# Two views, 64 bytes apart, of the normalised and inner rows of a two-block transformer kernel

## The chip, the cores and the metric

The kernel runs as one program on one core of a Trainium2 chip. The metric is device time in microseconds of one execution. The kernel before took 2518.12 us, the median of 3 runs that lay between 2514.95 and 2522.17 us.

## The reference, cut to what matters

All arithmetic is float32. There are 1024 model columns and 256 tokens per stream. A first block works on one stream ("b1" in the kernel). Two further layers ("l0", "l1") work on that stream and on a context stream of 256 tokens together, 512 tokens in all, until the last phases, in which the context is no longer needed. Each block is a gated feed-forward part, a mixer, and a second gated feed-forward part, each behind an RMS norm with modulation:

```python
D_MODEL = 1024; SEQ = 256; D_FF = 2816

def rmsnorm(x, g):
    xf = x.astype(jnp.float32)
    y = xf * lax.rsqrt(jnp.mean(xf * xf, axis=-1, keepdims=True) + NORM_EPS)
    return (y * g.astype(jnp.float32)).astype(x.dtype)
def modulate(x, shift, scale):
    return x * (1 + scale[:, None, :]) + shift[:, None, :]
def swiglu(x, w_gu, w_down):
    g, u = jnp.split(x @ w_gu, 2, axis=-1)
    return (jax.nn.silu(g) * u) @ w_down
...
    mod = c_act @ w_ada[l] + b_ada[l]
    (sh1, sc1, gt1, sh2, sc2, gt2, sh3, sc3, gt3) = jnp.split(mod, N_MOD, axis=-1)
    y = modulate(rmsnorm(h, norm_ffn1[l]), sh1, sc1)
    h = h + 0.5 * gt1[:, None, :] * swiglu(y, w_ffn1_gu[l], w_ffn1_down[l])
    y = modulate(rmsnorm(h, norm_mix[l]), sh2, sc2)
    proj = y @ w_in[l]
    ...  # attention and a gated MLP in b1, windowed attention and a long filter in l0, retention in l1
    h = h + gt2[:, None, :] * (merged @ w_out[l])
    y = modulate(rmsnorm(h, norm_ffn2[l]), sh3, sc3)
    h = h + 0.5 * gt3[:, None, :] * swiglu(y, w_ffn2_gu[l], w_ffn2_down[l])
```

Nearly all of the work is the products with the weight matrices: w_gu (1024 x 5632), w_down (2816 x 1024) twice per block, w_in and w_out.

## The kernel before, in words

Activations lie transposed in SBUF: 128 partitions are 128 model columns, and the free dimension is tokens. A product therefore has a 128 x 128 block of weights as its stationary operand and a row of 256 or 512 tokens as its moving operand, and its result goes to a PSUM tile (`pg`). To keep float32 accuracy with the faster float32r matmuls, every operand is split in two: a high part (`whi`, `Yh`, `Hh`) and the remainder (`wlo`, `Yl`, `Hl`). The helper `three` issues three matmuls for each block, one each at lines 1159, 1160 and 1161: high weights times high row, high weights times low row, low weights times high row. In the value blocks of the mixers the roles are exchanged (`three_moving`, lines 1335 to 1337): the weights are the moving operand with 256 columns, and 128 tokens of `Yh` or `Yl` are the stationary one.

The table `PHASES` orders the work in 18 phases, with a kind, a number of weight blocks and a number of tokens for each:

```python
PHASES = [
    ("b1_gu1", "t", 22, 256), ("b1_down1", "d", 16, 256),
    ("b1_in", "m", 10, 256), ("b1_out", "t", 4, 256),
    ("b1_gu2", "t", 22, 256), ("b1_down2", "d", 16, 256),
    ("l0_gu1", "t", 22, 512), ("l0_down1", "d", 16, 512),
    ("l0_in", "m", 12, 512), ("l0_out", "t", 4, 512),
    ("l0_gu2", "t", 22, 512), ("l0_down2", "d", 16, 512),
    ("l1_gu1", "t", 22, 512), ("l1_down1", "d", 16, 512),
    ("l1_in", "m", 24, 512), ("l1_out", "r", 8, 256),
    ("l1_gu2", "t", 22, 256), ("l1_down2", "d", 16, 256),
]
```

A block of kind "t" is 8 depth slices by 2 column halves by 3 matmuls, 48 in all; so are the blocks of the mixer inputs ("m", where a value block over 512 tokens has 96) and of "r". A block of kind "d" (`w_down`) is 11 depth slices by 3, 33 matmuls. "t" and "m" phases read the normalised rows `Yh` and `Yl` (8 rows of 512 columns each), "d" phases read the inner rows `Hh` and `Hl` (22 rows of 512 columns each), and l1_out reads `OH` and `OL`. A phase of 256 tokens uses the first 256 columns of a row. Every row starts 2048 bytes behind the one before it.

Weights travel so: SyncE issues the DMA of a block into one of two `raw` buffers (1 MB, or 704 KB for "d"), ScalarE rounds it to `whi` (lines 662, 667), VectorE subtracts to give `wlo` (lines 2049, 2054), and TensorE waits for `lo_ready`. ScalarE also writes `Yh` (line 710) and `Hh` (line 682), VectorE writes `Yl` (line 2209) and GpSimd `Hl` (line 526). Semaphore counts written out in each engine's program set the whole order; there is no scheduler. Between the weight blocks VectorE computes the modulation vectors from `w_ada` (line 2089).

Addresses: all tiles are laid out one behind another by `sb`, by hand. `X`, `Yh`, `Yl`, `raw`, `whi`, `wlo` and `ada` are multiples of 8192 bytes per partition. `V` (410 columns, 1664 bytes with its rounding), `MOD` (1728), and the small tiles up to `small` follow; `at[0] += 64` ahead of `region` makes up for `MOD`, so that `region`, with `Hh` and `Hl` in it, lies a multiple of 128 bytes behind `X`. Everything from line 241 on reuses `region` for the mixers (`over()` sets the address back).

Of the kernel before, what the change touches and what calls it, by code (L numbers as in the profile page):

```python
# [184 lines left out]

READS = {"b1_gu1": "b1_0", "b1_in": "b1_1", "b1_out": "merge", "b1_gu2": "b1_2", "l0_gu1": "l0_0", "l0_in": "l0_1",
# [3 lines left out]
def two_blocks(nc, x_t, ctx_t, vec, w_t, w_d, w_ada, emb_t, fw1, fw23, fw4, window, dft, rope1, sgu_w, sgu_b,  # L190
# [15 lines left out]
    Yh = sb("Yh", [P, 4096], F32R)  # L206
    Yl = sb("Yl", [P, 4096], F32R)
    raw = sb("raw", [P, 2, BLK])
# [18 lines left out]
    Hh = sb("Hh", [P, KF, 512], F32R)  # L227
    Hl = sb("Hl", [P, KF, 512], F32R)

# [4 lines left out]
    HF = nc.alloc_sbuf_tensor_at("HF", [P, 8, 512], F32, offset=y_at)[:, :, 256:512]  # L234
    DF0 = nc.alloc_sbuf_tensor_at("DF0", [P, 8, 512], F32, offset=y_at + 16384)[:, 2:6, 256:512]
    taps = nc.alloc_sbuf_tensor_at("HP", [P, 22, 512], F32, offset=region)
# [28 lines left out]
    over()  # L265
    k3_at = at[0]
# [28 lines left out]
    Yh8, Yl8, Yh16, Yl16 = rhs_t(Yh), rhs_t(Yl), rhs_r(Yh), rhs_r(Yl)  # L295
# [17 lines left out]
    with ExitStack() as ctx:  # L313
# [166 lines left out]
        def _(pool):  # L480
# [30 lines left out]
            def hidden_lo(name):  # L511

                tokens = INFO[name][2]
                k = FFNS.index(name) * KF
                if name == "b1_gu2":
                    for m in range(KF):
                        pool.wait_ge(sem["h_hi"], k + m + 1)
                        pool.tensor_tensor(Hl[:, m, 0:tokens], TMP[:, m % 2, 0:tokens], Hh[:, m, 0:tokens].bitcast(F32), ALU.subtract)\
                            .then_inc(sem["h_lo"], 1)
                        if m >= 4 and m < 19:  # L520
                            ctx_squares(m - 4)
                    return
                with pool.Fori(0, KF // 2) as j:
                    for u in range(2):
                        pool.wait_ge(sem["h_hi"], j * 2 + (k + u + 1))
                        pool.tensor_tensor(Hl[:, bass.ds(j * 2 + u, 1), 0:tokens], TMP[:, u:u + 1, 0:tokens],  # L526
                                           Hh[:, bass.ds(j * 2 + u, 1), 0:tokens].bitcast(F32), ALU.subtract)\
                            .then_inc(sem["h_lo"], 1)
# [107 lines left out]
        def _(act):  # L636
# [35 lines left out]
            def gate_evac(name):  # L672
# [4 lines left out]
                def evac(j, u):  # L677
# [4 lines left out]
                    act.activation(Hh[:, bass.ds(j * 2 + u, 1), 0:tokens], TMP[:, u:u + 1, 0:tokens], ACT.Copy)\  # L682
# [3 lines left out]
            def norm(name, chunks_of, tokens, shift, post, following=None):  # L686
# [20 lines left out]
                for c in range(k):  # L707
                    act.wait_ge(sem["scaled"], base + c + 1)
                    for s, cols in streams(tokens):
                        ins = act.activation(Yh8[:, c + post, cols], TMP[:, c % 2, cols], ACT.Identity, bias=shift(c, s)) \  # L710
                            if shift else act.activation(Yh8[:, c + post, cols], TMP[:, c % 2, cols], ACT.Copy)
# [5 lines left out]
            def lead_norm(name, shift, following):  # L717
# [8 lines left out]
                for c in range(k):  # L726
                    act.wait_ge(sem["lead_dve"], lead_dve(name, "scaled", c))
                    act.activation(Yh8[:, c, 0:256], TMP[:, c % 2, 0:256], ACT.Identity, bias=shift(c, 0)).then_inc(sem["lead_act"], 1)
# [15 lines left out]
            def rest_hi(name, shift, chunks):  # L744

                for c in chunks:
                    act.wait_ge(sem["scaled"], NORMS[name][1] + c + 1)
                    act.activation(Yh8[:, c, 256:512], TMP[:, c % 2, 256:512], ACT.Identity, bias=shift(c, 1)).then_inc(sem["y_hi"], 1)
# [219 lines left out]
            for c in range(8):  # L968
                act.wait_ge(sem["scaled"], base + c + 1)
                act.activation(Yh8[:, c, 0:256], TMP[:, c % 2, 0:256], ACT.Copy).then_inc(sem["y_hi"], 1)  # L970
# [184 lines left out]
        def _(pe):  # L1155
# [83 lines left out]
            def lead_products(name, u, n, signal):  # L1239

                def part(kt, half, cols):
                    w = slice(256 * kt + P * half, 256 * kt + P * half + P)
                    return three(pg[u][:, half, cols], whi[:, n % 2, w], wlo[:, n % 2, w], Yh8[:, kt, cols], Yl8[:, kt, cols], kt == 0, kt == 7)
# [13 lines left out]
            def lead_blocks(name, phase):  # L1257
# [9 lines left out]
                def other(kt, half, cols):  # L1267
                    w = slice(256 * kt + P * half, 256 * kt + P * half + P)
                    return three(pg[1][:, half, cols], whi[:, 1, w], wlo[:, 1, w], Yh8[:, kt, cols], Yl8[:, kt, cols], kt == 0, kt == 7)
# [13 lines left out]
            def product(name, first=0):  # L1283
# [4 lines left out]
                if mode == "d":  # L1288
                    h_before = KF * [f.replace("gu", "down") for f in FFNS].index(name) + CREDIT
# [212 lines left out]
            def b1_half(i):  # L1502
# [7 lines left out]
                for kt in range(8):  # L1510
                    if kind == "v":
                        w = slice(256 * kt, 256 * kt + 256)
                        y = slice(P * (i % 2), P * (i % 2) + P)
                        last = three_moving(out, whi[:, u, w], wlo[:, u, w], Yh8[:, kt, y], Yl8[:, kt, y], kt == 0, kt == 7)
                    else:
                        w = slice(256 * kt + P * (i % 2), 256 * kt + P * (i % 2) + P)
                        last = three(out, whi[:, u, w], wlo[:, u, w], Yh8[:, kt, 0:256], Yl8[:, kt, 0:256], kt == 0, kt == 7)
                last.then_inc(sem["b1_half"], 1)

            def b1_first_halves():  # L1520
# [3 lines left out]
                for kt in range(8):  # L1524
                    pe.wait_ge(sem["y_lo"], y_before("b1_1") + kt + 1)
                    for half in range(2):
                        w = slice(256 * kt + P * half, 256 * kt + P * half + P)
                        last = three(pg[0][:, half, 0:256], whi[:, b1_base % 2, w], wlo[:, b1_base % 2, w],
                                     Yh8[:, kt, 0:256], Yl8[:, kt, 0:256], kt == 0, kt == 7)
# [386 lines left out]
            def l1_block(b):  # L1916
# [12 lines left out]
                if kind == "v":  # L1929
                    for tt in range(4):  # L1930
                        out = pg[u][:, tt // 2, 256 * (tt % 2):256 * (tt % 2) + 256]
                        for kt in range(8):
                            w, y = slice(256 * kt, 256 * kt + 256), slice(P * tt, P * tt + P)
                            last = three_moving(out, whi[:, u, w], wlo[:, u, w], Yh8[:, kt, y], Yl8[:, kt, y], kt == 0, kt == 7)
                else:
                    tokens = 512 if kind == "k" else 256
                    for kt in range(8):
                        for half in range(2):
                            w = slice(256 * kt + P * half, 256 * kt + P * half + P)
                            last = three(pg[u][:, half, 0:tokens], whi[:, u, w], wlo[:, u, w],  # L1940
                                         Yh8[:, kt, 0:tokens], Yl8[:, kt, 0:tokens], kt == 0, kt == 7)
# [90 lines left out]
        def _(dve):  # L2032
# [160 lines left out]
            def norm(name, chunks_of, tokens, gain, shift, post, following=None):  # L2193
# [10 lines left out]
                def lo(c):  # L2204
                    dve.wait_ge(sem["y_hi"], yb + c + 1)
                    for s, cols in streams(tokens):
                        hi_part = Yh8[:, c + post, cols].bitcast(F32)
                        if shift:
                            ins = dve.scalar_tensor_tensor(Yl8[:, c + post, cols], TMP[:, c % 2, cols], shift(c, s), hi_part,  # L2209
                                                           ALU.add, ALU.subtract)  # L2210
                        else:
                            ins = dve.tensor_tensor(Yl8[:, c + post, cols], TMP[:, c % 2, cols], hi_part, ALU.subtract)
# [15 lines left out]
            def lead_norm(name, gate, gain, shift, following):  # L2228
# [8 lines left out]
                def lo(c):  # L2237
                    dve.wait_ge(sem["lead_act"], lead_act(name, "hi", c))
                    dve.scalar_tensor_tensor(Yl8[:, c, 0:256], TMP[:, c % 2, 0:256], shift(c, 0), Yh8[:, c, 0:256].bitcast(F32),
# [748 lines left out]
```

## Time and profile before

| | |
|---|---|
| median of 3 runs | 2518.12 us |
| the profiled execution's own time | 2518.71 us |
| its span | 2516.9 us |
| mean granted TensorE clock | 0.984 of 2.4 GHz |
| TensorE busy with matmuls | 2442.9 us (97%), 14736 matmuls |
| VectorE, ScalarE, GpSimd busy | 1515.5, 893.3, 380.7 us |
| share of the chain that ended last | TensorE 85%, VectorE 7%, ScalarE 3%, DMA 3% |

[...]

### The profile page before, as it was taken

How to read it: one execution, taken by the hardware profiler on the slowest of the kernel's cores; microseconds unless marked ns; L12 is line 12 of the kernel's file. 1: busy time of each engine (PE TensorE's matmuls, PEld its weight loads, DVE VectorE, ACT ScalarE, POOL GpSimd, SP SyncE). 2: the span in 40 equal slices, each digit the busy share in tenths (PEclk: the TensorE clock that was granted, in tenths of full speed). 3: DMA queues.
4: the chain of work that ended last, by engine and by line, in shares of the span. 5: the costliest groups of instructions: out<-in, count | busy, mean ns of one | idle time of the engine just before them, and what ended most of it. 6: DMA issues, size and time to landing. Idle time of an engine off the chain costs nothing.

```text
span 2516.9 us, 39335 instructions
## 1 busy us (share of the span) xinstructions
PE 2442.9 (97%) x14736; PEld 2165.5 (86%) x14736; DVE 1515.5 (60%) x2434; ACT 893.3 (35%) x1103; POOL 380.7 (15%) x353
## 2 busy tenths in 40 slices
PE   6999989999999998999999999999999999999999
PEld 5998879999888888867778888888888889999999
DVE  7676767967877765355477776642222364555444
ACT  4443554444222223332232222232222242254443
POOL 2110531211111102332211111001110001000110
PEclk7999989999999999999999999999999999999999
DMA  7877745854655554211135545422222342234545
GB/s 279 277 260 268 260 140 199 272 196 167 209 192 200 175 167 153 80 63 51 67 119 198 197 170 191 161 101 89 94 84 97 104 143 84 68 118 151 184 168 166
DMA packets 79878, 400.19 MB, mean 159 GB/s; under 512 B 8816, under 2 KB 12912, under 8 KB 54704
## 3 DMA queue, kind: packets, MB, share of 16 engines
q1 hardware_dynamic: 77216, 393.39, 45.3%
q0 software_dynamic: 1056, 3.67, 0.4%
q10 hardware_dynamic: 1520, 1.95, 0.2%
q8 instruction: 58, 0.95, 0.2%
q14 instruction: 28, 0.23, 0.0%
HBM read 396.88 MB, written 2.10 MB: 159 GB/s over the span
## 4 chain that ended last, share of the span: by engine, by line
PE 85%; DVE 7%; ACT 3%; DMA 3%; issue 2%; POOL 0%; ACTq 0%; SPq 0%; DVEq 0%; POOLq 0%
PE pg L1159 24%; PE pg L1161 24%; PE pg L1160 24%; DMA raw<-w_d 2%; PE pg L1335 2%; PE pg L1336 2%; PE pg L1337 2%; DVE wlo L2049 1%; PE px L1977 1%; DMA raw<-w_t 1%; ACT whi L662 1%; DVE ada L2089 1%; PE px L1738 1%; PE pg L1777 1%; PE px L1963 1%
## 5 line engine op out<-in xcount | busy, mean ns | idle before, releaser
L1159 PE MATMUL pg<-Yh,whi 128*128 128x256 f32 (+1 forms) x2856 | 958.6, 336 | 27.5 <-DVE Yl L2209 7.6
L1160 PE MATMUL pg<-Yl,whi 128*128 128x256 f32 (+1 forms) x2856 | 948.5, 332 | 0.0
L1161 PE MATMUL pg<-Yh,wlo 128*128 128x256 f32 (+1 forms) x2856 | 948.3, 332 | 0.0
L2054 DVE TENSOR_TENSOR wlo<-raw,whi 128x2048 fp32r<-128x2048 f32 (+1 forms) x202 | 415.0, 2055 | 517.7 <-ACT whi L667 517.0
L1159 PEld LDWEIGHTS pg<-Yh,whi 128*128 128x128 f32 x2856 | 548.0, 192 | 90.4 <-issue 20.9
L1161 PEld LDWEIGHTS pg<-Yh,wlo 128*128 128x128 f32 x2856 | 548.1, 192 | 50.1
L1160 PEld LDWEIGHTS pg<-Yl,whi 128*128 128x128 f32 x2856 | 548.4, 192 | 49.0
L667 ACT ACTIVATE whi<-raw 128x2048 fp32r<-128x2048 f32 (+1 forms) x202 | 348.4, 1725 | 563.8 <-PE pg L1161 521.8
L1159 PE MATMUL pg<-Hh,whi 128*128 128x256 f32 (+1 forms) x1122 | 368.9, 329 | 4.7 <-DVE wlo L2054 3.2
L1160 PE MATMUL pg<-Hl,whi 128*128 128x256 f32 (+1 forms) x1122 | 366.4, 327 | 0.0
L1161 PE MATMUL pg<-Hh,wlo 128*128 128x256 f32 (+1 forms) x1122 | 366.4, 327 | 0.0
L526 POOL TENSOR_TENSOR Hl<-TMP,Hh 128x512 f32 (+1 forms) x110 | 117.9, 1072 | 912.7 <-ACT Hh L682 912.7
L2089 DVE CUSTOM_DVE_ANT_0 ada<-ada,px 128x1024 f32<-128x1024 f32 x200 | 243.7, 1218 | 13.9 <-DMA ada<-w_ada 8.5
L1159 PEld LDWEIGHTS pg<-Hh,whi 128*128 128x128 f32 x1122 | 213.2, 190 | 25.6 <-DVE wlo L2054 5.1
L1160 PEld LDWEIGHTS pg<-Hl,whi 128*128 128x128 f32 x1122 | 213.3, 190 | 18.1
L1161 PEld LDWEIGHTS pg<-Hh,wlo 128*128 128x128 f32 x1122 | 213.3, 190 | 17.9
L2049 DVE TENSOR_TENSOR wlo<-raw,whi 128x2048 fp32r<-128x2048 f32 (+1 forms) x65 | 132.9, 2044 | 115.6 <-ACT whi L662 115.5
L662 ACT ACTIVATE whi<-raw 128x2048 fp32r<-128x2048 f32 (+1 forms) x63 | 107.7, 1709 | 237.0 <-PE pg L1161 116.7
L682 ACT ACTIVATE Hh<-TMP 128x256 f32 (+3 forms) x132 | 69.4, 525 | 341.9 <-DVE TMP L2162 341.9
L568 POOL TENSOR_TENSOR wlo<-raw,whi 128x512 fp32r<-128x512 f32 x88 | 111.9, 1302 | 177.1 <-ACT whi L982 124.7
L495 POOL TENSOR_TENSOR TMP<-TMP,SQ 128x512 f32<-128x512 f32 (+1 forms) x54 | 58.7, 1088 | 387.2 <-ACT SQ L773 322.5
L2086 DVE CUSTOM_DVE_ANT_0 RS<-ada,px,small 128x512 f32<-128x512 f32 x144 | 107.7, 748 | 5.1
(352 smaller groups left out, 2354.8 us busy)
## 6 DMA issues: line engine op xcount, KB each, us to landing
raw<-w_t SPq DMA_DIRECT2D x194, 1024.0 KB, 5.0
ada<-w_ada SPq DMA_DIRECT2D x200, 512.0 KB, 3.6
raw<-w_d SPq DMA_DIRECT2D x96, 704.0 KB, 4.1
ADA<-w_ada SPq DMA_DIRECT2D x16, 512.0 KB, 14.6
NB<-na_bias POOLq DMA_DIRECT2D x8, 256.0 KB, 2.9
X<-x_t ACTq DMA_DIRECT2D x2, 512.0 KB, 16.7
spectrum<-HF POOLq DMA_DIRECT2D x1, 1024.0 KB, 9.2
X<-ctx_t SPq DMA_DIRECT2D x1, 1024.0 KB, 7.4
```

The source lines that it names most:

```text
L526: pool.tensor_tensor(Hl[:, bass.ds(j * 2 + u, 1), 0:tokens], TMP[:, u:u + 1, 0:tokens], Hh[:, bass.ds(j * 2 + u, 1), 0:tokens].bitcast(F32 ...
L568: ins = pool.tensor_tensor(wlo[:, n % 2, part], raw[:, n % 2, part], whi[:, n % 2, part].bitcast(F32), ALU.subtract)
L662: act.activation(whi[:, n % 2, 0:size], raw[:, n % 2, 0:size], ACT.Copy).then_inc(sem["hi_ready"], 1)
L667: act.activation(whi[:, n % 2, 0:size], raw[:, n % 2, 0:size], ACT.Copy).then_inc(sem["hi_ready"], 1)
L682: act.activation(Hh[:, bass.ds(j * 2 + u, 1), 0:tokens], TMP[:, u:u + 1, 0:tokens], ACT.Copy)\
L1159: pe.matmul(out, w_hi, y_hi, start=first, stop=False)
L1160: pe.matmul(out, w_hi, y_lo, start=False, stop=False)
L1161: return pe.matmul(out, w_lo, y_hi, start=False, stop=last)
L2049: dve.tensor_tensor(wlo[:, n % 2, 0:size], raw[:, n % 2, 0:size], whi[:, n % 2, 0:size].bitcast(F32), ALU.subtract)\
L2054: dve.tensor_tensor(wlo[:, n % 2, 0:size], raw[:, n % 2, 0:size], whi[:, n % 2, 0:size].bitcast(F32), ALU.subtract)\
L2086: summed(dve.tensor_tensor_reduce(RS[:, :], ada[:, n % 2, 512:1024], px[1][:, 1, :], 1.0, part, ALU.mult, ALU.add, total[:, 0:1]), 2)
L2089: summed(dve.tensor_tensor_reduce(w, w, px[2 - streams][:, :, :], 1.0, 0.0, ALU.mult, ALU.add, total[:, streams - 1:streams]), 1 if stream ...
```

## The change

`Yh`, `Yl`, `Hh` and `Hl` each get a second view, 64 bytes further on (`YhB`, `YlB`, `HhB`, `HlB`). `row_view` and `inner_of` give the later view to the phases of 256 columns (and to the whole of l1_in, whose key blocks have 512 columns), and the earlier view to the others. The tiles of the l1 mixer, `OH` and `OL` among them, begin 64 bytes later as well, and so do the tiles of the filter taps (`HF`, `DF0`, `HP`). 128 bytes of padding stand behind `Yh`, `Yl` and `Hh`, 64 behind `Hl`; what follows moves by 128 or 256 bytes. No instruction is added, removed or moved on any engine, and no semaphore count changes.

```diff
+SHORT_ROWS = ("b1_0", "b1_gu1", "b1_1", "b1_in", "merge", "b1_out", "b1_2", "b1_gu2", "l1_1", "l1_in", "l1_2", "l1_gu2")
...
     y_at = at[0]
     Yh = sb("Yh", [P, 4096], F32R)
+    YhB = nc.alloc_sbuf_tensor_at("YhB", [P, 4096], F32R, offset=y_at + 64)
+    at[0] += 128
+    yl_at = at[0]
     Yl = sb("Yl", [P, 4096], F32R)
+    YlB = nc.alloc_sbuf_tensor_at("YlB", [P, 4096], F32R, offset=yl_at + 64)
+    at[0] += 128
...
     Hh = sb("Hh", [P, KF, 512], F32R)
+    HhB = nc.alloc_sbuf_tensor_at("HhB", [P, KF, 512], F32R, offset=region + 64)
+    at[0] += 128
+    hl_at = at[0]
     Hl = sb("Hl", [P, KF, 512], F32R)
+    HlB = nc.alloc_sbuf_tensor_at("HlB", [P, KF, 512], F32R, offset=hl_at + 64)
+    at[0] += 64
+    assert at[0] <= end
...
-    HF = nc.alloc_sbuf_tensor_at("HF", [P, 8, 512], F32, offset=y_at)[:, :, 256:512]
+    HF = nc.alloc_sbuf_tensor_at("HF", [P, 8, 512], F32, offset=y_at + 64)[:, :, 256:512]
...
     over()
+    at[0] += 64
     k3_at = at[0]
...
+    def row_view(name):
+        return (YhB8, YlB8) if name in SHORT_ROWS else (Yh8, Yl8)
+    def inner_of(name):
+        return (HhB, HlB) if INFO[name][2] == 256 else (Hh, Hl)
...
                                     last = three(pg[v][:, 0, 0:tokens], whi[:, half, w], wlo[:, half, w],
-                                                 Hh[:, 11 * half + kt, 0:tokens], Hl[:, 11 * half + kt, 0:tokens],
+                                                 inner_hi[:, 11 * half + kt, 0:tokens], inner_lo[:, 11 * half + kt, 0:tokens],
                                                  half == 0 and kt == 0, half == 1 and kt == 10)
...
                                 last = three(pg[u][:, half, 0:tokens], whi[:, u, w], wlo[:, u, w],
-                                             Yh8[:, kt, 0:tokens], Yl8[:, kt, 0:tokens], kt == 0, kt == 7)
+                                             row_view(name)[0][:, kt, 0:tokens], row_view(name)[1][:, kt, 0:tokens], kt == 0, kt == 7)
```

The writers (ScalarE, VectorE, GpSimd) and every other reader of these rows get the same replacement.

## Rows read from the trace of the kernel before

**Rows 1.** The page: chain that ended last, by engine and by line.
```profile
PE 85%; DVE 7%; ACT 3%; DMA 3%; issue 2%; POOL 0%; ACTq 0%; SPq 0%; DVEq 0%; POOLq 0%
```
**Rows 2.** PE by stretch: us, busy (x records), granted clock, DMA share, GB/s.
```profile
60.00:100.00 40.00, 40.00 (x335) 1.00 0.82 278
60.00:180.00 120.00, 120.00 (x1002) 1.00 0.78 269
640.00:700.00 60.00, 60.00 (x266) 1.00 0.61 210
640.00:940.00 300.00, 300.00 (x1325) 1.00 0.55 188
2360.00:2400.00 40.00, 40.00 (x336) 1.00 0.51 179
2360.00:2480.00 120.00, 120.00 (x1003) 1.00 0.51 175
190.00:250.00 60.00, 55.35 (x428) 1.00 0.78 267
250.00:420.00 170.00, 153.47 (x1074) 0.92 0.54 192
```
**Rows 3.** Matmul groups by shape, whole run: line, names, shapes, count, busy, mean ns.
```profile
L1160 PE MATMUL pg<-Yl,whi 128*128 128x256 f32 x1584 | 453.4, 286 | 0.0
L1160 PE MATMUL pg<-Hl,whi 128*128 128x256 f32 x660 | 186.7, 283 | 0.0
L1337 PE MATMUL pg<-whi,Yl 128*128 128x256 f32 x352 | 99.6, 283 | 0.0
L1160 PE MATMUL pg<-OL,whi 128*128 128x256 f32 x128 | 36.2, 283 | 0.0
```
**Rows 4.** Timeline of PE just after a wait: start us, length us, instruction.
```profile
272.43 0.35 PE L1159 MATMUL pg<-Yh,whi 128*128 128x256 f32 x1 [1.20 <-POOL wlo L568]
272.62 0.28 PE L1160 MATMUL pg<-Yl,whi 128*128 128x256 f32 x1
272.74 0.28 PE L1161 MATMUL pg<-Yh,wlo 128*128 128x256 f32 x1
272.85 0.28 PE L1159 MATMUL pg<-Yh,whi 128*128 128x256 f32 x1
272.97 0.28 PE L1160 MATMUL pg<-Yl,whi 128*128 128x256 f32 x1
...
273.45 0.28 PE L1161 MATMUL pg<-Yh,wlo 128*128 128x256 f32 x1
```
**Rows 5.** Timeline of PE at a block's boundary in b1_gu1.
```profile
54.40 0.29 PE L1159 MATMUL pg<-Yh,whi 128*128 128x256 f32 x1
54.53 0.28 PE L1160 MATMUL pg<-Yl,whi 128*128 128x256 f32 x1
54.66 0.29 PE L1161 MATMUL pg<-Yh,wlo 128*128 128x256 f32 x1
54.78 0.28 PE L1159 MATMUL pg<-Yh,whi 128*128 128x256 f32 x1
```
**Rows 6.** Timeline of PE before 51 us, at the lower granted clock.
```profile
48.75 0.41 PE L1159 MATMUL pg<-Yh,whi 128*128 128x256 f32 x1
...
50.46 0.41 PE L1161 MATMUL pg<-Yh,wlo 128*128 128x256 f32 x1
```
**Rows 7.** Timeline of PE in the l1 mixer: ten float32 matmuls, merged.
```profile
2194.98 2.32 PE L1977 MATMUL px<-G,VN 128*128 128x256 f32 x10
```
**Rows 8.** Weight loads (PEld) by shape in 60:190 us.
```profile
L1160 PEld LDWEIGHTS pg<-Yl,whi 128*128 128x128 f32 x321 | 61.6, 192 | 0.0
```
**Rows 9.** The same in 640:940 us, beside matmuls of 512 columns.
```profile
L1161 PEld LDWEIGHTS pg<-Yh,wlo 128*128 128x128 f32 x300 | 56.3, 188 | 11.6
```
**Rows 10.** The chain that ended last, in order of time, in b1_down1.
```profile
210.19 5.68 DMA raw<-w_d
215.97 1.39 ACT whi L667
217.38 1.64 DVE wlo L2054
219.18 5.57 DMA raw<-w_d
```
**Rows 11.** Waits of ScalarE in 60:170 us: us in total, times, longest us.
```profile
ACT whi L667 <- PE pg L1161: 12.2, 19, 0.7
```

More of the change, by code:

```diff
@@ L709, in norm @@
                     for s, cols in streams(tokens):
-                        ins = act.activation(Yh8[:, c + post, cols], TMP[:, c % 2, cols], ACT.Identity, bias=shift(c, s)) \
-                            if shift else act.activation(Yh8[:, c + post, cols], TMP[:, c % 2, cols], ACT.Copy)
+                        ins = act.activation(row_view(name)[0][:, c + post, cols], TMP[:, c % 2, cols], ACT.Identity, bias=shift(c, s)) \
+                            if shift else act.activation(row_view(name)[0][:, c + post, cols], TMP[:, c % 2, cols], ACT.Copy)
                     ins.then_inc(sem["y_hi"], 1)
@@ L727, in lead_norm @@
                     act.wait_ge(sem["lead_dve"], lead_dve(name, "scaled", c))
[L728 removed]
+                    act.activation(row_view(name)[0][:, c, 0:256], TMP[:, c % 2, 0:256], ACT.Identity, bias=shift(c, 0)).then_inc(sem["lead_act"], 1)
                     if c == 3:
@@ L747, in rest_hi @@
                     act.wait_ge(sem["scaled"], NORMS[name][1] + c + 1)
-                    act.activation(Yh8[:, c, 256:512], TMP[:, c % 2, 256:512], ACT.Identity, bias=shift(c, 1)).then_inc(sem["y_hi"], 1)
+                    act.activation(row_view(name)[0][:, c, 256:512], TMP[:, c % 2, 256:512], ACT.Identity, bias=shift(c, 1)).then_inc(sem["y_hi"], 1)
             def squares(name):
@@ L1242, in part @@
                     w = slice(256 * kt + P * half, 256 * kt + P * half + P)
-                    return three(pg[u][:, half, cols], whi[:, n % 2, w], wlo[:, n % 2, w], Yh8[:, kt, cols], Yl8[:, kt, cols], kt == 0, kt == 7)
+                    return three(pg[u][:, half, cols], whi[:, n % 2, w], wlo[:, n % 2, w], row_view(name)[0][:, kt, cols], row_view(name)[1][:, kt, cols], kt == 0, kt == 7)
                 for kt in range(8):
@@ L1268, in other @@
                     w = slice(256 * kt + P * half, 256 * kt + P * half + P)
-                    return three(pg[1][:, half, cols], whi[:, 1, w], wlo[:, 1, w], Yh8[:, kt, cols], Yl8[:, kt, cols], kt == 0, kt == 7)
+                    return three(pg[1][:, half, cols], whi[:, 1, w], wlo[:, 1, w], row_view(name)[0][:, kt, cols], row_view(name)[1][:, kt, cols], kt == 0, kt == 7)
                 for kt in range(8):
@@ L1513, in b1_half @@
                         y = slice(P * (i % 2), P * (i % 2) + P)
-                        last = three_moving(out, whi[:, u, w], wlo[:, u, w], Yh8[:, kt, y], Yl8[:, kt, y], kt == 0, kt == 7)
+                        last = three_moving(out, whi[:, u, w], wlo[:, u, w], row_view("b1_in")[0][:, kt, y], row_view("b1_in")[1][:, kt, y], kt == 0, kt == 7)
                     else:
                         w = slice(256 * kt + P * (i % 2), 256 * kt + P * (i % 2) + P)
-                        last = three(out, whi[:, u, w], wlo[:, u, w], Yh8[:, kt, 0:256], Yl8[:, kt, 0:256], kt == 0, kt == 7)
+                        last = three(out, whi[:, u, w], wlo[:, u, w], row_view("b1_in")[0][:, kt, 0:256], row_view("b1_in")[1][:, kt, 0:256], kt == 0, kt == 7)
                 last.then_inc(sem["b1_half"], 1)
@@ L1528, in b1_first_halves @@
                         last = three(pg[0][:, half, 0:256], whi[:, b1_base % 2, w], wlo[:, b1_base % 2, w],
-                                     Yh8[:, kt, 0:256], Yl8[:, kt, 0:256], kt == 0, kt == 7)
+                                     row_view("b1_in")[0][:, kt, 0:256], row_view("b1_in")[1][:, kt, 0:256], kt == 0, kt == 7)
                         if kt == 7:
@@ L1933, in l1_block @@
                             w, y = slice(256 * kt, 256 * kt + 256), slice(P * tt, P * tt + P)
-                            last = three_moving(out, whi[:, u, w], wlo[:, u, w], Yh8[:, kt, y], Yl8[:, kt, y], kt == 0, kt == 7)
+                            last = three_moving(out, whi[:, u, w], wlo[:, u, w], row_view("l1_in")[0][:, kt, y], row_view("l1_in")[1][:, kt, y], kt == 0, kt == 7)
                 else:
@@ L1940, in l1_block @@
                             last = three(pg[u][:, half, 0:tokens], whi[:, u, w], wlo[:, u, w],
-                                         Yh8[:, kt, 0:tokens], Yl8[:, kt, 0:tokens], kt == 0, kt == 7)
+                                         row_view("l1_in")[0][:, kt, 0:tokens], row_view("l1_in")[1][:, kt, 0:tokens], kt == 0, kt == 7)
                 last.then_inc(sem["pe_block"], 1)
```

30 lines of the change are left out of this document (16 added, 14 removed).

## The prediction

> **What bounds the kernel now.** I read the chain of work that ended last before all else, since busy shares say little in an engine that overlaps its own work. TensorE holds 85% of it, and no other engine more than 7% [rows 1]. So the price of one matmul decides, and the record's length does not give it, because records overlap. I took it from the counts in two windows that differ by a known stretch. In the 256-column phases 120 us hold 667 more records than 40 us: 80,000 / 667 = 119.94 ns from start to start. In the last phase, the same lengths again give 667. The DMA share is 0.78 in the first and 0.51 in the last, so the load of the DMA engines does not set this period. With 512 columns it is 240,000 / 1059 = 226.6 ns [rows 2].
>
> At the full granted clock, 2.4 GHz, 256 columns take 106.7 ns and 512 take 213.3 ns. Both periods therefore lie 13.3 ns above the streaming time. At the lower level, 1.2 GHz, eight matmuls from 48.75 to 50.46 us are 213.8 ns apart [rows 6], which is 256 / 1.2 and nothing more: the 13.3 ns show only at the full clock. The float32 matmuls of the l1 mixer stream 256 columns twice. Ten of them take 2.32 us, and with a record of 0.379 us for the last, nine distances of 215.7 ns: 2.4 ns above 213.3 [rows 7]. So the engine can start a matmul 2.4 ns behind the last column of the one before; the float32r ones do not.
>
> **Is any of the 13.3 ns movable by an address?** Two rows say a part may be. First, the period of 256-column matmuls is not always 119.94 ns. After a wait, the starts at 272.62, 272.74, 272.85 and 272.97 are 117 ns apart on average, and seven distances up to 273.45 average 118.6 ns [rows 4]. Operands, shapes and clock are those of the steady stretch. Something takes hold after a few matmuls and costs some 2.5 ns each. Second, a weight load has a record of 192 ns beside 256-column matmuls and 188 ns beside 512-column ones [rows 8, 9], though both load the same 128 x 128 block. The stream of the row and the load of the next weights start within nanoseconds of each other and read the same memory at addresses that all agree modulo 128 bytes: by the code `Yh`, `Yl`, `Hh`, `Hl`, `whi` and `wlo` are multiples of 128 behind one another, and their slices step by 512 or 2048 bytes. The change shifts one of the two streams by 64 bytes in the 256-column phases and leaves the 512-column phases, in which the load is not stretched, as they are. That is a case for a gain, not a proof: no float32r row of before starts at another phase.
>
> A rule of the Trainium skill speaks against this reading. "TensorE: Matmul & The Clock Gate", Part 2, step 1, has it that the moving operand and the weight load have independent read ports, and that loading weights takes no bandwidth from the running matmul. By that rule the two records would be alike; the 192 beside the 188 ns [rows 8, 9] do not agree with it. With it the sum would be nothing, 2518 us.
>
> **Part by part.** No instruction comes, goes or moves, so no wait and no queue changes; only addresses do.
>
> (a) Moving operands shifted by 64 bytes. From the phase table: b1_gu1 and b1_gu2 22 x 48 = 1056 each; b1_down1 and b1_down2 16 x 33 = 528 each; b1_in without its two value blocks 8 x 48 = 384; b1_out 192; l1_in's four q and eight g blocks 576; l1_out 384; l1_gu2 1056; l1_down2 528. Sum 6288, out of 3 x (1584 + 660 + 128) = 7116 records with a row of 256 columns [rows 3]; the rest belong to 512-token phases that work in halves.
>
> Of these, b1_down1 (528) and b1_in (384) stand between waits. In 190 to 250 us TensorE is busy only 55.35 of 60 us, in 250 to 420 us 153.47 of 170 [rows 2]. In b1_down1 the chain runs through load, rounding and subtraction (5.68 + 1.39 + 1.64 us, then the next load) without TensorE [rows 10], so a shorter matmul there only lengthens the wait. That leaves 5376 on the path. In b1_gu1, beside the highest DMA share, ScalarE waits for TensorE before each rounding, 12.2 / 19 = 0.64 us [rows 11]. A block that is 48 x 2.4 ns = 0.12 us shorter stays under that, so the loads are next but not yet late.
>
> Price of one: bounded below by the float32 row, which would make the period 106.7 + 2.4 = 109.1 ns, a gain of 10.8 ns, 5376 x 10.8 = 58 us. Bounded above by the longest distances that stand in a row without a wait: 54.40 to 54.78 us, three distances of 126.7 ns [rows 5], a loss of 6.8 ns, 37 us on 5376. I take 117.5 ns, what the engine does before the slower pattern takes hold [rows 4], between the 117 of the first three distances and the 118.6 of seven: a gain of 2.44 ns. 5376 x 2.44 = 13.1 us.
>
> (b) Value blocks of b1_in and l1_in: 96 + 768 = 864 matmuls keep the weights as their moving operand and now load `Yh` or `Yl` from the shifted view. Their record is like the others' (283 ns, [rows 3]). If the phase between the two streams is what matters they gain 2.44 ns as well, 2.1 us; if the row's own start does, nothing. I take nothing.
>
> (c) The key blocks of l1_in, 4 x 48 = 192 matmuls of 512 columns, read the shifted view. By the ends of (a), 10.8 ns gained to 6.8 lost, they are worth -2.1 to +1.3 us; I take 0, as [rows 9] show nothing stretched there.
>
> (d) The 128 and 256 bytes of padding move `whi`, `wlo`, `raw`, `ada` and the rest by multiples of 128. For the 512-column phases this keeps every phase modulo 128 (`Yl` and `Hl` change modulo 256 against `Yh`). Nothing in the rows separates 128 from 256; bounds as in (a) on 5202 matmuls of 512 columns would be -56 to +35 us. I take 0, because the only pattern that I see is the one of the shared phase, and I leave this inside the range.
>
> (e) float32 matmuls of the l1 mixer with operands 64 bytes later: already at 2.4 ns above streaming [rows 7], so a gain is at most 2.4 ns each, under 1 us for about 300. Writes of ScalarE, VectorE and GpSimd to shifted rows: their time is hidden behind TensorE except in the norms, where a chunk is 0.4 to 0.5 us; I take 0.
>
> Sum: -13.1 us against the profiled execution's own 2518.71 us (span 2516.9), 0.6 us above the median of the runs. From the median: 2518.1 - 13.1 = 2505 us.
>
> **Rivals.** *Nothing changes.* The start address is immaterial at this grain; 117 ns after a wait is only a queue being refilled, and 192 beside 188 ns a matter of overlap. For it: the steady period is 119.94 in three tiles alike (`Yh`, `Hh`, `OH`), and no row shows an address at work. Time 2518 us. The Trainium skill's "SBUF — State Buffer" page, section on the DMA port swizzle, knows only 16-byte lines, which a shift by 64 bytes does not touch; by that rule, too, the time stays at 2518 us. No row here separates it from this rival.
>
> *A deep gain.* Most of the 13.3 ns is a matter of the start address, and the period falls to 109 to 115 ns. For it: the float32 row at 2.4 ns. Against it: the 512-column period carries the same 13.3 ns though its weight load is not stretched, so the bulk looks like a fixed cost of float32r. At 112 ns, 5376 x 7.9 = 43 us, 2475 us; less if the rounding in the b1 phases then comes late, since 48 x 7.9 = 0.38 us nears the 0.64 of [rows 11].
>
> *The loads take it back.* The 2.44 ns are there, but in b1_gu1, b1_gu2 and b1_down2 (2640 matmuls) the weights become the bound as in b1_down1. What is left is 2736 x 2.44 = 6.7 us: 2511 us. Against it: the 0.64 us of slack.
>
> *Slower.* The shifted row meets the weight load in a worse phase, or spans one more line of memory at each end, and the period rises to the 126.7 ns of [rows 5] in the shifted phases: +37 us on the 5376, 2555 us. It decides from 121.3 ns on (1.4 ns x 5376 = 7.6 us). For it: such distances exist. Against it: they are three in a row at one block's boundary, after which 120 returns.
>
> **How the numbers follow.** A difference under 0.3%, 7.6 us, is about what a measurement of this kernel cannot tell from none. Chances: the forecast 0.38 (its own range 2498 to 2512), deep gain 0.17, nothing 0.27, taken back 0.05, slower 0.13. Nearly all of the first two is faster than 2510.5 us: 0.54. Within 0.3%: the rest of the forecast, nothing and taken back, 0.33. Slower 0.13. The range 2470 to 2524 us leaves out the far end of the deep gain, with the bounds of (d) that go with it, and most of the slower case.
>
> **What would show it.** Right: in 60 to 180 us against 60 to 100 us, about 681 more records in place of 667 (117.5 ns), the same in 2360 to 2480, and in 640 to 940 still 1059. The weight load's mean falls from 192 to 188 ns. The waits in b1_down1 grow by what its matmuls lose. Wrong: 667 again (nothing), over 700 (deep), under 660 (slower), or another count in the 512-column window, which would mean that the padding acts by itself.

## The result, and the profile after

The changed kernel took 2526.94 us (median of 20 runs, 2519.0 to 2533.61) against 2518.22 us (2511.2 to 2524.24) for the kernel before on the same chips: a ratio of 1.0034, 95% interval 1.0024 to 1.0044. It is slower by 0.34%, where 2505 us was forecast, and 3 us above the range of 2470 to 2524 us. The profiled execution has a span of 2529.4 us, 12.5 us more than before.

The chain that ended last is still TensorE's, with the shares of the page's row that answers to [rows 1]:

```profile
PE 81%; DVE 8%; issue 4%; DMA 3%; ACT 3%; POOL 0%; DVEq 0%; ACTq 0%; SPq 0%; POOLq 0%
```

So the price of one matmul decides here too. It is read from one start to the next: a record of 256 columns is 283 to 286 ns long [rows 3], but the starts lie 119.94 ns apart, so records overlap. That distance is called the period below. Next the windows, with the same bounds as [rows 2] and two more: us, PE busy (x records), granted clock, DMA share, GB/s.

```profile
60.00:100.00 40.00, 40.00 (x342) 1.00 0.82 278
60.00:180.00 120.00, 120.00 (x1019) 1.00 0.80 273
640.00:700.00 60.00, 60.00 (x261) 1.00 0.56 193
640.00:940.00 300.00, 300.00 (x1299) 1.00 0.53 183
2360.00:2400.00 40.00, 40.00 (x342) 1.00 0.52 185
2360.00:2480.00 120.00, 120.00 (x1022) 1.00 0.51 176
...
1340.00:1380.00 40.00, 40.00 (x173) 1.00 0.55 194
1340.00:1600.00 260.00, 260.00 (x1116) 1.00 0.53 182
```

By the same differences of counts, the 256-column period is 80,000 / 677 = 118.2 ns in b1_gu1 and 80,000 / 680 = 117.6 ns in l1_gu2 with the first part of l1_down2 (2360 to 2480 us), where [rows 2] give 119.94. The 512-column period is 240,000 / 1038 = 231.2 ns in l0_gu1 and l0_down1, where [rows 2] give 226.6, and 220,000 / 943 = 233.3 ns in the stretch from 1340 to 1600 us. In that last stretch the kernel before had this:

```profile
1340.00:1380.00 40.00, 40.00 (x179) 1.00 0.56 188
1340.00:1600.00 260.00, 260.00 (x1149) 1.00 0.54 184
```

That is 220,000 / 970 = 226.8 ns. So both kinds of phases changed their period, the one down and the other up, with the same instructions at the same granted clock.

The weight loads of the changed kernel answer to [rows 8] and [rows 9]: the first two rows are of 60 to 190 us, the last of 640 to 940 us (count, busy us, mean ns, idle before).

```profile
L1183 PEld LDWEIGHTS pg<-YlB,whi 128*128 128x128 f32 x319 | 60.3, 189 | 0.0
L1184 PEld LDWEIGHTS pg<-YhB,wlo 128*128 128x128 f32 x319 | 59.9, 188 | 0.0
...
L1184 PEld LDWEIGHTS pg<-Yh,wlo 128*128 128x128 f32 x291 | 54.6, 188 | 12.7
```

The 192 ns beside 256 columns are gone, as forecast. But beside 512 columns the load is at 188 ns as before, while the period rose by 4.6 ns and more. It is 188 ns from 1340 to 1600 us too, beside the period of 233.3 ns:

```profile
L1183 PEld LDWEIGHTS pg<-Yl,whi 128*128 128x128 f32 x268 | 50.4, 188 | 11.3
```

The length of the load's record does not tell whether the pair of streams is at its best.

All 14736 matmuls have a record in each trace and their order is the same, so matmul number n of one trace is matmul n of another. The time between the same matmuls, in us, worked out from their starts (the stretches are named by the kernel before's time; their bounds are the same matmuls in every column; e1 and e2 are experiments, below):

```
stretch (us of before)   columns        before   after   change   e1_pad256  e2_pad_only
46 to 190, b1_gu1        256             144.0   141.7     -2.3       141.4        141.5
190 to 400               256, waits      210.1   207.8     -2.3       210.5        210.9
400 to 513, b1_gu2       256             112.9   111.4     -1.5       111.1        110.1
513 to 600, b1_down2     256              87.2    87.3     +0.1        85.7         86.2
600 to 950, l0           512             349.8   355.7     +5.9       349.6        355.9
1000 to 1270, l0 mixer   512, float32    270.6   274.8     +4.2       270.6        273.0
1330 to 1610, l0         512             279.9   288.2     +8.3       279.9        288.2
1670 to 1980, l1         512             310.1   319.2     +9.1       310.1        313.1
2080 to 2270, l1 mixer   256, turned     190.0   184.7     -5.3       185.8        189.0
2320 to 2513, l1         256             191.8   188.3     -3.5       189.0        189.2
```

(A stretch bears the name of the phase that fills most of it; "turned" matmuls are those with the weights as the moving operand.) The phases of 512 columns lost 27.5 us in the four stretches shown; the phases of 256 columns gained 14.8. The short stretches left out make up the rest of the 12.5.

### The profile page after: what moved, and what is told of

The parts are those of the page before. It is cut to its first block, busy times and chain, and to the rows that moved or that the text cites. A ratio compares the mean times of both kernels' runs of the same rounds, so it can differ in the third digit from the quotient of the medians.

```text
span 2529.4 us, 39335 instructions
## 1 busy us (share of the span) xinstructions
PE 2451.6 (97%) x14736; PEld 2146.4 (85%) x14736; DVE 1514.1 (60%) x2434; ACT 892.5 (35%) x1103; POOL 381.0 (15%) x353
## 4 chain that ended last, share of the span: by engine, by line
PE 81%; DVE 8%; issue 4%; DMA 3%; ACT 3%; POOL 0%; DVEq 0%; ACTq 0%; SPq 0%; POOLq 0%
PE pg L1182 23%; PE pg L1184 23%; PE pg L1183 23%; PE pg L1359 2%; DMA raw<-w_d 2%; PE pg L1360 1%; PE pg L1361 1%; DMA raw<-w_t 1%; DVE wlo L2073 1%; PE px L2001 1%; ACT whi L685 1%; DVE ada L2113 1%; ACT whi L690 1%; PE px L1762 1%; PE pg L1801 1%
## 5 line engine op out<-in xcount | busy, mean ns | idle before, releaser
L1182 PE MATMUL pg<-Yh,whi 128*128 128x512 f32 (+1 forms) x1352 | 524.0, 388 | 10.6 <-DVE Yl L2301 2.6
L1183 PE MATMUL pg<-Yl,whi 128*128 128x512 f32 (+1 forms) x1352 | 517.4, 383 | 0.0
L1184 PE MATMUL pg<-Yh,wlo 128*128 128x512 f32 (+1 forms) x1352 | 516.3, 382 | 0.0
L1182 PE MATMUL pg<-YhB,whi 128*128 128x256 f32 (+1 forms) x1504 | 438.5, 292 | 18.7 <-DVE YlB L2233 7.6
L1184 PE MATMUL pg<-YhB,wlo 128*128 128x256 f32 (+1 forms) x1504 | 434.8, 289 | 0.0
L1183 PE MATMUL pg<-YlB,whi 128*128 128x256 f32 (+1 forms) x1504 | 430.3, 286 | 0.0
L1182 PEld LDWEIGHTS pg<-Yh,whi 128*128 128x128 f32 x1352 | 255.2, 189 | 71.3 <-issue 6.2
L1184 PEld LDWEIGHTS pg<-Yh,wlo 128*128 128x128 f32 x1352 | 255.2, 189 | 55.6
L1183 PEld LDWEIGHTS pg<-Yl,whi 128*128 128x128 f32 x1352 | 255.5, 189 | 51.0
L1183 PEld LDWEIGHTS pg<-YlB,whi 128*128 128x128 f32 x1504 | 287.7, 191 | 2.8
```

The lines of the kernel that those rows point to most:

```text
L1182: pe.matmul(out, w_hi, y_hi, start=first, stop=False)
L1183: pe.matmul(out, w_hi, y_lo, start=False, stop=False)
L1184: return pe.matmul(out, w_lo, y_hi, start=False, stop=last)
```

## The experiments

**e1_pad256: the padding made 256 bytes.**

```diff
-    at[0] += 128
+    at[0] += 256
```

(at its three places, behind `Yh`, `Yl` and `Hh`)

> The changed kernel with 256 bytes of padding behind Yh, Yl and Hh in place of 128, so that the low rows lie where they did before against the high rows and the weights, modulo 256. Theory A: the 512-column phases of the changed kernel are slower (231.2 against 226.6 ns a matmul) because Yl and Hl moved by 128 bytes modulo 256 against Yh, Hh and the weights. It expects 226.6 ns in 640 to 940 us and, with the 256-column phases at 117.5 to 118.2 ns as in the changed kernel, 2503 to 2508 us. Theory B: the 512-column phases are slower for another reason (where tiles lie beyond 256 bytes, the second views in the address map). It expects 231 ns there again and about 2527 us.

Measured: 2503.62 us (2499.19 to 2513.72, 7 runs), ratio to before 0.9952, interval 0.9935 to 0.9969. Its windows:

```profile
60.00:100.00 40.00, 40.00 (x342) 1.00 0.82 281
60.00:180.00 120.00, 120.00 (x1022) 1.00 0.79 274
640.00:700.00 60.00, 60.00 (x267) 1.00 0.59 209
640.00:940.00 300.00, 300.00 (x1326) 1.00 0.55 189
```

240,000 / 1059 = 226.6 ns, exactly the count of [rows 2], and 80,000 / 680 = 117.6 ns. In the table above its 512-column stretches are those of before to 0.2 us. Theory A holds: what slowed them was the low row's place modulo 256 bytes. The second views without that are worth some 12 us, near the 13.1 that the prediction gave them; what they are made of stands under step (a) below.

**e2_pad_only: the padding of 128 bytes without the views.**

```diff
     def row_view(name):
-        return (YhB8, YlB8) if name in SHORT_ROWS else (Yh8, Yl8)
+        return (Yh8, Yl8)
     def inner_of(name):
-        return (HhB, HlB) if INFO[name][2] == 256 else (Hh, Hl)
+        return (Hh, Hl)
```

(and `HF`, `DF0`, `HP` and the l1 mixer back to their former starts)

> The changed kernel with the padding of 128 bytes alone: all phases use the earlier view, HF, DF0, HP and the l1 mixer start where they did. Theory A expects 231 ns in the 512-column phases, so about 24 us more than before there, and 120 ns or slightly more in the 256-column phases: 2538 to 2550 us. Theory B, by which the padding is harmless, expects 226.6 and 119.9 ns: 2518 us.

Measured: 2533.96 us (2530.4 to 2540.23, 6 runs), ratio 1.0073, interval 1.0056 to 1.0089; a little under the range that theory A gave, since that range had the 256-column phases at 120 ns.

```profile
60.00:100.00 40.00, 40.00 (x342) 1.00 0.82 285
60.00:180.00 120.00, 120.00 (x1021) 1.00 0.79 274
640.00:700.00 60.00, 60.00 (x261) 1.00 0.60 209
640.00:940.00 300.00, 300.00 (x1300) 1.00 0.54 185
1700.00:1740.00 40.00, 40.00 (x177) 1.00 0.27 99
1700.00:1960.00 260.00, 260.00 (x1138) 1.00 0.26 92
```

The 512-column period is 240,000 / 1039 = 231.0 ns: the loss comes with the padding alone. From 1700 to 1960 us it is only 220,000 / 961 = 228.9 ns, where the changed kernel, with the same addresses of rows and weights, has 233.3. So the address alone does not fix it; e7 takes this up. Not expected was the other side: with the low row 128 bytes off, the 256-column phases run at 80,000 / 679 = 117.8 ns, no worse than with the views. Since the padding alone gives that period, the 256-column gain of the changed kernel can't be put down to its views. What they add there is mostly in the turned matmuls of the l1 mixer, where e2_pad_only needs 189.0 us and the changed kernel 184.7.

**e3_all_late: the later view in every phase.**

```diff
-    at[0] += 128
+    at[0] += 256
... (at its three places)
-    Yh8, Yl8, YhB8, YlB8 = rhs_t(Yh), rhs_t(Yl), rhs_t(YhB), rhs_t(YlB)
+    YhB8, YlB8 = rhs_t(YhB), rhs_t(YlB)
+    Yh8, Yl8, Hh, Hl = YhB8, YlB8, HhB, HlB
```

> 256 bytes of padding, and the later view (64 bytes on) in every phase, the 512-column ones too. If a shift of 64 bytes between row and weights is good whatever the number of columns, the 512-column period falls from 226.6 to about 224 ns and the time to about 2495 us. If the shift is good for 256 columns only, the 512-column period rises to 228 ns or more: above 2510 us. Its 256-column phases should equal those of e1_pad256 (117.5 to 118.2 ns).

Measured: 2512.47 us (2507.8 to 2517.59, 12 runs), ratio 0.9983, interval 0.9973 to 0.9993.

```profile
640.00:700.00 60.00, 60.00 (x264) 1.00 0.59 207
640.00:940.00 300.00, 300.00 (x1312) 1.00 0.54 186
```

240,000 / 1048 = 229.0 ns: 64 bytes are good for 256 columns and bad for 512. Its 256-column period in 60 to 180 us is that of e1_pad256 (80,000 / 679 = 117.8 ns). So the choice of a view by the number of columns is sound; it was the padding that spoiled it.

**e4_table: the disputed cost by itself.** One kernel with no other engine at work while TensorE runs, 38 sets of 96 matmuls, three per weight block as in `three`; M has the weights as the moving operand, as in `three_moving`.

```diff
+SETS = [(n, *o) for n in (256, 512) for o in (
+    (0, 0, 0, 0), (1, 1, 0, 0), (2, 2, 0, 0), (3, 3, 0, 0), (4, 4, 0, 0), (5, 5, 0, 0), (6, 6, 0, 0), (7, 7, 0, 0),
+    (2, 2, 2, 2), (1, 1, 1, 1), (0, 2, 0, 0), (2, 4, 6, 6), (3, 5, 6, 6), (0, 0, 0, 2), (0, 1, 0, 0), (1, 3, 0, 0))]
+SETS += [("M", *o) for o in ((0, 0, 0, 0), (1, 1, 0, 0), (2, 2, 0, 0), (3, 3, 0, 0), (3, 5, 6, 6), (2, 4, 6, 6))]
```

> Not the computation: 38 sets of 96 matmuls (three per weight block, as in the kernel), with no other engine at work, each set with its own start addresses of high row, low row, high weights and low weights; its output is not the reference's. Theory A expects 120.0 ns for 256 columns and 226.7 for 512 where all four starts agree, 117.5 to 118.5 ns for 256 columns with the rows 64 bytes off the weights, and about 231 ns for 512 columns where the low row is 128 bytes off the high one (0,2,0,0), with a pattern that repeats after 256 bytes: (4,4,0,0) like (0,0,0,0). Theory B expects 226.7 ns for 512 columns in all sets. If it is the start of the row by itself that counts, (2,2,2,2) and (1,1,1,1) differ from (0,0,0,0); if only the distance counts, they are equal to it.

Measured, the period in ns over the last 48 matmuls of each set, worked out from their starts (high row, low row, high weights, low weights, each in steps of 64 bytes; every set was entered once):

```
starts           256 columns   512 columns     M (weights moving)
0 0 0 0             120.0         226.7          120.0
1 1 0 0             117.8         228.8          113.3
2 2 0 0             118.7         233.4          118.6
3 3 0 0             113.3         233.4          117.8
4 4 0 0             120.0         226.7
5 5 0 0             117.7         228.8
6 6 0 0             118.7         233.4
7 7 0 0             113.3         233.4
1 1 1 1             120.0         226.7
2 2 2 2             120.0         226.7
0 2 0 0             117.8         233.4
2 4 6 6             117.8         233.4          119.1   (512 columns of the changed kernel)
3 5 6 6             117.8         230.3          113.3   (256 columns of the changed kernel)
0 0 0 2             119.1         231.0
0 1 0 0             117.8         231.7
1 3 0 0             117.8         230.3
```

Six of its windows: 256 columns at 64 and at 192 bytes (10 us each), 512 columns at 0 and at (0,2,0,0) (20 us each), and M at 0 and at 64 bytes (10 us each):

```profile
37.00:47.00 10.00, 10.00 (x88) 1.00 0.00 0
61.00:71.00 10.00, 10.00 (x90) 1.00 0.01 2
218.00:238.00 20.00, 20.00 (x90) 1.00 0.00 1
446.00:466.00 20.00, 20.00 (x87) 1.00 0.00 1
584.00:594.00 10.00, 10.00 (x86) 1.00 0.01 2
596.00:606.00 10.00, 10.00 (x91) 1.00 0.00 0
```

The counts order the sets as the periods do, with two or three records more than the period gives, since records overlap the bounds. The DMA column shows that nothing else moves. With theory A everything fits but the last digit: the pattern repeats after 256 bytes, only the distances between rows and weights count and not the row's own place (1 1 1 1 and 2 2 2 2 are like 0 0 0 0, and 1 3 0 0 is like 3 5 6 6), and 512 columns are best at distance 0, where 256 columns are at their worst. The value for the low row 128 bytes off is 233.4, above the 231 that was expected; e7 shows why both occur.

**e5_table16: the same in steps of 16 bytes.**

```diff
+SETS = [(n, k, k, 0, 0) for n in (256, 512) for k in (0, 1, 2, 3, 4, 6, 8, 10, 11, 12, 13, 14, 15)]
+SETS += [(n, *o) for n in (256, 512) for o in (
+    (12, 0, 0, 0), (0, 12, 0, 0), (12, 12, 0, 4), (12, 12, 0, 12), (12, 8, 0, 0), (0, 0, 0, 4), (0, 0, 0, 12))]
```

> Not the computation: the table again, in steps of 16 bytes, and with high and low rows or weights apart; its output is not the reference's. The first table gave, for rows 0, 64, 128 and 192 bytes behind the weights, 120.0, 117.8, 118.7 and 113.3 ns at 256 columns and 226.7, 228.8, 233.4 and 233.4 ns at 512. Theory A1, a conflict between lines of 64 bytes: every start within 0 to 63 bytes reads like 0, those within 192 to 255 like 192. Theory A2, it is the exact distance in time of the two streams: the values between change from one 16-byte step to the next, and 512 columns may have a better start than 0.

Measured, the period in ns, with both rows moved by the step and one entry for each:

```
step of 16 bytes      0      1      2      3      4      6      8     10     11     12     13     14     15
256 columns       120.0  113.3  116.6  118.3  117.8  120.0  118.7  117.3  119.2  113.3  119.2  118.4  117.0
512 columns       226.7  231.7  233.3  233.4  229.0  233.2  232.2  234.3  233.3  233.3  234.6  233.4  233.3
```

Theory A1 falls: 16 bytes change the period as much as 64 do (231.7 against 226.7 ns at 512 columns). For 512 columns no start tried is better than 0, and none of the sets with rows or weights apart is either (228.9 to 234.5 ns).

**e6_192: the rows of the 256-column phases 192 bytes on, l1_in at 64.** Like e1_pad256, but:

```diff
-    HhB = nc.alloc_sbuf_tensor_at("HhB", [P, KF, 512], F32R, offset=region + 64)
+    HhB = nc.alloc_sbuf_tensor_at("HhB", [P, KF, 512], F32R, offset=region + 192)
...
-        return (YhB8, YlB8) if name in SHORT_ROWS else (Yh8, Yl8)
+        if name in ("l1_1", "l1_in"):
+            return YhB8, YlB8
+        return (YhC8, YlC8) if name in SHORT_ROWS else (Yh8, Yl8)
```

(`YhC` and `YlC` are views 192 bytes on; `HlB`, the tiles of the filter taps and those of the l1 mixer start 192 bytes on as well)

> e1_pad256 with the rows of the 256-column phases 192 bytes behind the weights instead of 64; in l1_in, where 768 of the matmuls have the weights as moving operand, 64 bytes are kept. Theory A, by the first table: 113.3 instead of 117.7 ns on the matmuls that TensorE's path holds outside l1_in, 5376 - 576 = 4800 of them, so 21 us less than e1_pad256: 2482 us. If the b1 phases then meet the loads (48 x 4.4 ns = 0.21 us a block, 0.33 us with what e1_pad256 already took, against a slack of 0.64 us), 2488 to 2492 us. If the table's value does not hold with other engines at work, 2503 us.

Measured: 2501.23 us (2492.02 to 2506.68, 6 runs), ratio 0.9924, interval 0.9903 to 0.9946, which overlaps that of e1_pad256. Both beat both kernels. The 2482 us did not come. Five windows of 20 us, in b1_gu1, twice in b1_gu2, in l1_gu2 and in l1_down2, and one of 120 us in the first phase:

```profile
120.00:140.00 20.00, 20.00 (x179) 1.00 0.81 287
440.00:460.00 20.00, 20.00 (x172) 1.00 0.87 286
480.00:500.00 20.00, 20.00 (x172) 1.00 0.84 282
2320.00:2340.00 20.00, 20.00 (x172) 1.00 0.54 203
2465.00:2485.00 20.00, 20.00 (x179) 1.00 0.60 197
60.00:180.00 120.00, 118.87 (x1037) 1.00 0.81 277
```

179 records are the 113.3 ns of the table and 172 are 117.8 ns. From the starts, nearly all of b1_gu2 and l1_gu2, and l1_down2 up to 2452 us, run at 117.8, most of b1_gu1 and the rest of l1_down2 at 113.3: at the same distance of rows and weights, and without regard to the DMA share. In these phases each change between the two stands right behind a short wait of TensorE. Here is the one in l1_down2, a window before it, the timeline's line of the wait, and a window behind it:

```profile
2440.00:2450.00 10.00, 10.00 (x87) 1.00 0.51 161
2452.89 0.38 PE L1186 MATMUL pg<-HhB,whi 128*128 128x256 f32 x1 [0.20 <-DVE wlo L2082]
2460.00:2470.00 10.00, 10.00 (x90) 1.00 0.55 170
```

Where the fast period did come, waits of TensorE took most of it back: the 1178 distances from 46 to 190 us of before take 140.1 us here and 141.4 in e1_pad256, although b1_gu1's period is some 4 ns shorter. The waits among them, distances of over 150 ns from start to start, hold 6.0 us beyond the period here and 2.8 in e1_pad256. The turned matmuls of l1_in, with the rows at 64 bytes in both, had 116.7 ns on average, and 115.1 in e1_pad256.

**e7_entries: is it the address alone?** The table again, with each pair of starts entered four or six times after slightly different pauses.

```diff
+SETS = [(256, k, k, 0, 0) for k in (0, 1, 4, 8, 12, 15) for _ in range(6)]
+SETS += [(512, k, l, 0, 0) for k, l in ((0, 0), (4, 4), (0, 8)) for _ in range(4)]
+SETS += [(256, 0, 8, 0, 0) for _ in range(6)]
```

> Not the computation: sets of 96 matmuls again, each pair of starts entered four or six times after pauses of slightly different length; its output is not the reference's. In e6_192 stretches at 113.3 ns alternated with stretches at 117.8 ns, at the same addresses. Theory C1: the period is one of a few steady patterns (120.0, 117.8, 113.3 ns), and the entry decides which, within what the addresses allow. It expects 12 steps (192 bytes) and 1 step (16 bytes) to come out at 113.3 in some entries and near 117.8 in others, 0 steps at 120.0 always. Theory C2: the address alone decides, and the stretches at 117.8 ns in e6_192 come from the other engines. It expects the same period in all entries of a set, 113.3 for 12 steps and 1 step, 117.8 for 4.

```
columns, starts (16 bytes)    period in each entry, ns
256,  0  0                    120.0  120.0  120.0  120.0  120.0  120.0
256,  1  1                    113.3  116.6  120.0  118.7  118.7  118.7
256,  4  4                    117.8  117.8  117.7  117.8  117.8  117.8
256,  8  8                    118.7  118.7  118.6  118.7  118.6  118.6
256, 12 12                    113.3  117.8  113.3  113.3  113.3  113.3
256, 15 15                    117.2  117.2  117.2  117.2  117.2  117.2
256,  0  8                    117.8  117.8  117.8  117.7  117.8  117.8
512,  0  0                    226.7  226.7  226.7  226.7
512,  4  4                    228.9  229.0  229.0  228.8
512,  0  8                    233.4  231.1  231.1  231.1
```

Two windows of 10 us, in the first and the second entry at 192 bytes:

```profile
316.00:326.00 10.00, 10.00 (x91) 1.00 0.01 2
328.00:338.00 10.00, 10.00 (x87) 1.00 0.00 0
```

Theory C1 holds in the main: with no other engine at work, the same addresses gave different periods. Some distances had one period in all their entries (0, 64, 128 and 240 bytes and the low row 128 bytes off at 256 columns, 0 and 64 at 512); 192 and 16 bytes had several, and the entry, that is, the way in which a stretch starts after a pause, picks one that then stays for the rest of the set. At 16 bytes there were four, from 113.3 to 120.0 ns, more than C1 had named. At 192 bytes the second entry settled at the 117.8 ns that e6_192 shows in b1_gu2. The low row 128 bytes off gives 233.4 or 231.1 ns at 512 columns, and these are the two periods of the changed kernel: 231.2 ns in 640 to 940 us, 233.3 in 1340 to 1600. The 228.9 ns that e2_pad_only had at this distance is a third, which no entry here picked. Nor does a period always last until the next wait: in e2_pad_only it went from 233.3 to 231.1 ns near 632 us, in the middle of a steady stretch. So the values of e4 and e5, of one entry each, are what a distance can give, not what it must.

## Why the prediction was wrong

*What bounds the kernel, and the price of one matmul.* Right. TensorE's period decided, and the sums by periods meet the trace: the 280 us from 1330 to 1610 hold some 1235 matmuls of 226.7 ns, 1235 x 6.5 ns are 8.0 us, and the stretch lost 8.3.

*Step (a), the shifted rows.* Right in that a shift of 64 bytes between row and weights shortens the period: to 117.8 ns in e4_table, where 117.5 was forecast and the changed kernel has 117.6 to 118.2. The size is right in part by luck. e1_pad256, which has this step without the shift of the low row against the high one, is 0.9952 of before, some 12 us less on 2516, where 13.1 were forecast. But 768 x (119.9 - 115.1) = 3.7 us of this are the turned matmuls of step (b), taken at nothing, so the step itself gave 8 to 9. The 117.5 ns were read from the first distances behind a wait at equal addresses [rows 4]. No run links these to the steady period at 64 bytes (every entry of e7_entries at equal addresses settled at 120.0), so that the size came out so near is luck as well. That the wait in b1_down1 and b1_in takes the gain there fits e1_pad256 (210.1 us before, 210.5 there, from 190 to 400) but not the changed kernel, which gained 2.3 us in that stretch. That the same 256-column period comes from the padding alone (e2_pad_only) was not foreseen.

*Step (b), the turned matmuls.* Mis-sized. They were taken at nothing, or at 2.44 ns if the distance of the two streams is what matters. The distance does matter, and turned round (the weights moving, the rows 64 bytes later) it is the good one: 113.3 ns in e4_table. The stretch from 2080 to 2270 us holds 768 of them and gained 5.3 us. From the starts, their period went from 119.9 to 113.5 ns, which is 4.9 us; another 384 matmuls in it, not turned, went from 120.0 to 117.8, 0.8 us.

*Steps (c) and (e), taken at nothing.* The 192 key-block matmuls of l1_in went from 227.7 to 230.4 ns, a loss of 0.5 us, inside the bounds given. The float32 matmuls of the l1 mixer went from 215.9 to 216.4 ns, so nothing was gained there. That they stream their columns twice fits: in the trace of before the float32 periods are 109, 215.7 and 429 ns for 128, 256 and 512 columns, each twice the columns at 2.4 GHz and some 2.4 ns.

*Step (d), the padding.* This is the step that failed. The prediction said that nothing in the rows separates 128 from 256 bytes and took 0, "because the only pattern that I see is the one of the shared phase". By the code the rows and the weights of before agree modulo 256 bytes, not only modulo 128 as the prediction put it: the small tiles ahead of `region`, with the 64 bytes added, come to 15,104 bytes, 59 x 256, and the large ones are multiples of 8192. The pattern repeats after 256 bytes, so 128 bytes of padding put `Yl` and `Hl` at the farthest distance from the weights and raised the 512-column period from 226.6 to 231.2 and 233.3 ns. The changed kernel and e1_pad256 differ in the padding alone: 1.0034 against 0.9952 of before, some 21 us. In e2_pad_only the padding without the views costs 0.73% (18 us at the ratio), net of what it gains at 256 columns. The bound that the prediction gave for it, +35 us on 5202 matmuls, held the 27.5 us that were lost, but the bound went neither into a rival nor into the range beyond a few us, so that the range ended at 2524.

*The reading of the weight load.* The prediction left the 512-column phases out because their load was not stretched (188 ns). The same 188 ns stand beside 226.6 and beside 233.3 ns. An absent symptom was read as an absent mechanism. The rule quoted from the Trainium skill ("TensorE: Matmul & The Clock Gate", Part 2, step 1), that the weight load takes nothing from the running matmul, does not sit well with e4_table either: with no other engine at work, the distance of the two addresses alone moved the period between 113.3 and 120.0 ns. Whether the reads are where the two meet, no run shows.

*The rivals.* "Slower" was given 0.13, but for another mechanism, worse 256-column rows; e1_pad256 excludes that one. "Nothing changes", and with it the 16-byte line as a reason for it, is excluded by the table. "The loads take it back" is near but not reached: in 60 to 170 us of the changed kernel ScalarE waits for TensorE less, and now for a load now and then (us in total, times, longest; against [rows 11]):

```profile
ACT whi L690 <- PE pg L1184: 6.3, 13, 0.6
ACT whi L690 <- DMA raw<-w_t: 4.0, 4, 1.3
```

In e6_192, with its shorter period, waits did take most of the gain of b1_gu1 back.

*What stays open.* What in the chip makes the period depend on the distance, and why an entry settles where it does, is not shown; that two streams of reads collide is only argued. e7_entries shows that no other engine is needed for two periods at one address; whether other engines take part in the choice, as in e6_192 and e2_pad_only, stays open. The changed kernel's runs spread over 14.6 us, the kernel before's over 13.0, so the spread is no sign of the several periods. Every period given for a whole kernel is of one traced execution.

## What to carry to other kernels

Where TensorE is the bound and every matmul loads its own weights (float32r here; no other type was tried), the starts of the moving and of the stationary operand relative to each other are a tuning knob, and its good setting depends on the number of columns. Measure it in a small kernel with nothing else at work, several entries per setting, and prefer a setting that gives one period in all of them. A shorter period is worth its full size only where no wait grows by it (e6_192). Padding is part of the edit: check what it does to every tile behind it against every tile that it is read with, by the full length of the pattern (256 bytes here), and give an edit whose cost no row shows a rival of its own.

## What the runs showed of the hardware that was not expected

- The start-to-start time of float32r matmuls at the full granted clock depends on the distance of row and weights: 113.3 to 120.0 ns at 256 columns, 226.7 to 234.6 at 512 (e4_table, e5_table16). In steps of 64 bytes it repeats after 256 (e4_table).
- At equal addresses it is exactly 120.0 ns at 256 columns and 226.7 at 512; 113.3 and 226.7 are 272 and 544 cycles of 2.4 GHz.
- At some distances the period is one of several steady patterns, picked at the entry: six entries at 192 bytes gave 113.3 five times and 117.8 once (e7_entries). In e6_192 the changes between the two that were looked at followed a wait of TensorE; in e2_pad_only one came without (233.3 to 231.1 ns near 632 us).
